# Decoder layer on one core: first two column tiles of the projection multiplied in token halves between the transposes of x

## What is computed

```python
hn = rms_norm(x, mix_norm_w[l])          # x: 1024 x 1024
proj = hn @ w_in[l]                      # w_in: 1024 x 2560
q, k, v, xr, gr = jnp.split(proj, splits, axis=-1)
...                                      # attention on q, k, v; gated recurrence on xr, gr
x = x + jnp.concatenate([att, rnn], axis=-1) @ w_out[l]
hn = rms_norm(x, ffn_norm_w[l])
x = x + hier_moe(hn, ...)                # 32 experts, two for each token
return rms_norm(x, final_norm_w)
```

## Time and profile before

| | us |
|---|---|
| three runs | 1178.47, 1175.91, 1177.88 (median 1177.88) |
| the profiled execution | 1176.9 |
| its span | 1174.8 |
| TensorE busy | 1056.3 (90% of the span) |
| VectorE busy | 878.4 (75%) |
| ScalarE busy | 729.8 (62%) |
| chain of waits, TensorE's share | 59% |
| mean clock granted to TensorE | 0.944 of full |

### The profile page before, as it was taken

How to read it: one execution, slowest core, us unless ns; L and a number is a source line. 1 busy time by engine, 2 the same in 40 slices (tenths; PEclk the granted TensorE clock), 3 DMA queues, 4 the chain that set the end, 5 groups by cost and what they waited for, 6 DMA issues and landing times.

```text
span 1174.8 us, 15610 instructions
## 1 busy us (share of the span) xinstructions
PE 1056.3 (90%) x5171; PEld 870.6 (74%) x5171; DVE 878.4 (75%) x1287; ACT 729.8 (62%) x953; POOL 130.7 (11%) x162
## 2 busy tenths in 40 slices
PE   4899999997777799994999999999999999999950
PEld 3788777786565688883888888888888888888830
DVE  6311266505778777768799999999999999999977
ACT  6222465615656832223688888888888888888824
POOL 1000000000000100001021221221221211211110
PEclk7899999998889999995999999999999999999985
DMA  7111111100004164457599999999999999999577
GB/s 230 52 57 50 37 36 36 36 1 0 1 1 146 21 260 139 144 227 259 214 401 389 375 382 389 381 390 385 366 391 376 370 411 367 385 401 377 226 308 286
DMA packets 49526, 273.27 MB, mean 233 GB/s; under 512 B 12016, under 2 KB 22416, under 8 KB 37200
## 3 DMA queue, kind: packets, MB, share of 16 engines
q1 hardware_dynamic: 40144, 255.72, 55.6%
q0 software_dynamic: 9344, 17.06, 3.9%
HBM read 255.97 MB, written 33.55 MB: 246 GB/s over the span
## 4 chain that ended last, share of the span: by engine, by line
PE 59%; DVE 4%; DMA 1%; issue 0%; ACT 0%; SPq 0%; POOL 0%; POOLq 0%; DVEq 0%
PE ps_moe L68 18%; PE ps_moe L70 17%; PE ps_moe L72 17%; PE ps_moe L1382 2%; PE ps_moe L1184 1%; PE ps_moe L1406 1%; DVE qkvT L1777 1%; DVE gate_up L1754 1%; DVE w_lo L1347 1%; DMA y_d<-y_sb,y_entry 1%; DMA y_second<-y_d 1%; PE ps_moe L1174 1%; PE ps_moe L1167 0%; DVE wout_lo L977 0%; PE ps_moe L1234 0%
## 5 line engine op out<-in xcount | busy, mean ns | idle before, releaser
L1347 DVE TENSOR_TENSOR w_lo<-qkvT,w_hi 128x1024 fp32r<-128x1024 f32 x192 | 224.0, 1224 | 3.7 <-ACT w_hi L1343 1.2
L1343 ACT ACTIVATE w_hi<-qkvT 128x1024 fp32r<-128x1024 f32 x192 | 192.7, 1056 | 15.9 <-PE ps_moe L72 15.9
L68 PE MATMUL ps_moe<-w_hi,x_hi 128*128 128x512 f32 x512 | 162.6, 399 | 4.1 <-DVE x_lo L1391 4.1
L70 PE MATMUL ps_moe<-w_lo,x_hi 128*128 128x512 f32 x512 | 159.3, 392 | 0.0
L72 PE MATMUL ps_moe<-w_hi,x_lo 128*128 128x512 f32 x512 | 158.8, 391 | 0.0
L1347 DVE TENSOR_TENSOR w_lo<-gate_up,w_hi 128x1024 fp32r<-128x1024 f32 x128 | 148.1, 1224 | 2.3 <-ACT w_hi L1343 0.4
L1343 ACT ACTIVATE w_hi<-gate_up 128x1024 fp32r<-128x1024 f32 x128 | 126.4, 1056 | 4.9 <-PE ps_moe L72 4.9
L70 PEld LDWEIGHTS ps_moe<-w_lo,x_hi 128*128 128x128 f32 x512 | 96.9, 189 | 20.9
L72 PEld LDWEIGHTS ps_moe<-w_hi,x_lo 128*128 128x128 f32 x512 | 96.7, 189 | 21.0
L68 PEld LDWEIGHTS ps_moe<-w_hi,x_hi 128*128 128x128 f32 x512 | 94.7, 190 | 22.2 <-DVE x_lo L1391 4.5
L333 DVE TENSOR_TENSOR q_parts<-w_raw,k_parts 128x1024 fp32r<-128x1024 f32 x16 | 19.6, 1224 | 91.9 <-ACT k_parts L233 91.9
(11 more groups left out here) (255 smaller groups left out, 1880.0 us busy)
## 6 DMA issues: line engine op xcount, KB each, us to landing
qkvT<-in_w_exp_gate SPq DMA_DIRECT2D x16, 2048.0 KB, 10.3
qkvT<-in_w_exp_up SPq DMA_DIRECT2D x16, 2048.0 KB, 15.2
gate_up<-in_w_exp_gate SPq DMA_DIRECT2D x16, 2048.0 KB, 10.6
gate_up<-in_w_exp_up SPq DMA_DIRECT2D x16, 2048.0 KB, 15.4
qkvT<-in_w_exp_down SPq DMA_DIRECT2D x16, 2048.0 KB, 14.5
down<-in_w_exp_down SPq DMA_DIRECT2D x16, 2048.0 KB, 14.7
w_raw<-in_w_in SPq DMA_DIRECT2D x10, 1024.0 KB, 5.2
hn_d<-qkvT SPq DMA_DIRECT2D x16, 512.0 KB, 3.8
```

What stands on the lines that cost most here:

```text
L68: nc_mm(o, lh, rh[h], start=start, stop=False)
L70: nc_mm(o, lh, rl[h], start=False, stop=False)
L1343: act.activation(two(w_hi, r), raw_unit(u, par), ACT.Copy).then_inc(q.split_high, 1)
L1347: dve.tensor_tensor(two(w_lo, r), raw_unit(u, par), two(w_hi, r).bitcast(F32), ALU.subtract).then_inc(q.split_low, 1)
```

## The change

1. The load of the norm row moves from SyncE's queue to ScalarE's, ahead of everything that ScalarE does.
2. ScalarE takes one root of a constant before its first square.
3. On ScalarE and VectorE the loops over the x tiles are unrolled. The high and low part of the first weight tile are made behind high and low part 2 of x, those of the second weight tile behind high and low part 4.
4. TensorE transposes x tiles 0 to 4, and then waits for low part 3 (tokens 0 to 511) and the first weight tile. Behind transposes 4 and 5 it multiplies column tile 1 by the first token half, four inner slices (12 products) each time; behind transposes 6 and 7 the same for column tile 2. After the row transpose it multiplies both by the second token half, 24 products each. From the third column tile on the work is as before, its loop of two rounds written out.

The change to lines:

```diff
--- before.py
+++ after.py
@@ -150,7 +150,6 @@
         def _(sp):
             for c in range(2):
                 sp.dma_start(x_sb(c), io["x"][0][c * P:(c + 1) * P, :]).then_inc(x_in[c], 16)
-            sp.dma_start(norm_w[:, :], io["mix_norm_w"][0].partition_broadcast(P)).then_inc(norm_w_in, 16)
             with sp.Fori(1, TT // 2) as i:
                 for c in range(2):
 
@@ -211,7 +210,10 @@
         @block.scalar
         def _(act):
             link = Link(act, act_own)
+            act.dma_start(norm_w[:, :], io["mix_norm_w"][0].partition_broadcast(P)).then_inc(norm_w_in, 16)
             act.wait_ge(ident0, 3)
+
+            link(act.activation(stat[:, 1, 0:1], eps[:, 0:1], ACT.Sqrt))
 
             def square(i, c):
                 act.wait_ge(x_in[c], i * 16 + 16)
@@ -255,21 +257,18 @@
 
             square(0, 0)
             square(0, 1)
-            with act.Fori(0, TT // 2 - 1) as i:
-                link.loop(i, 2)
-                for c in range(2):
-                    square(i + 1, c)
-                    high(i, c)
-            link.end(TT // 2 - 1)
-            split_high((0, 16), 0)
-            high(TT // 2 - 1, 0)
-            high(TT // 2 - 1, 1)
+            for n in range(TT):
+                if n + 2 < TT:
+                    square((n + 2) // 2, n % 2)
+                high(n // 2, n % 2)
+                if n in (2, 4):
+                    split_high((n // 2 - 1, 16), n // 2 - 1)
             act.wait_ge(chan_ready, 2)
             act.activation(soft[:, 2, :], soft[:, 1, :], ACT.Exp, scale=-1.0).then_inc(exp_ready, 1)
-            with act.Fori(0, 2) as i:
-                for c in range(4):
-                    split_high((i * 4 + (c + 1), i * 16 + (16 + 16 * (c == 3))), (c + 1) % 4)
-                    evacuate(i * 4 + c, mixT[:, bass.ds(i * 4 + c, 1)].rearrange("p o n -> p (o n)"), c)
+            for tile in range(8):
+                if tile:
+                    split_high((tile + 1, 16 * ((tile + 1) // 4 + 1)), (tile + 1) % 4)
+                evacuate(tile, mixT[:, tile], tile % 4)
             for i in range(2):
                 for c in range(4):
                     tile = 8 + i * 4 + c
@@ -319,15 +318,6 @@
                                   hT_hi[:, :, at].bitcast(F32), ALU.subtract).then_inc(lo_out, 1)
 
             dve.wait_ge(norm_w_in, 16)
-            scale(0, 0)
-            scale(0, 1)
-            with dve.Fori(0, TT // 2 - 1) as i:
-                link.loop(i, 2)
-                for c in range(2):
-                    scale(i + 1, c)
-                    low(i, c)
-            link.end(TT // 2 - 1)
-
             def split_low(n, c):
                 dve.wait_ge(w_hi_ready, n)
                 ins = dve.tensor_tensor(w_lo[:, c % 2], w_raw[:, c // 2, :, (c % 2) * P:(c % 2 + 1) * P],
@@ -363,9 +353,14 @@
                 dve.tensor_tensor(gate, gate, r_sb[:, :], ALU.mult).then_inc(lru_done, 1)
 
 
-            split_low(1, 0)
-            low(TT // 2 - 1, 0)
-            low(TT // 2 - 1, 1)
+            scale(0, 0)
+            scale(0, 1)
+            for n in range(TT):
+                if n + 2 < TT:
+                    scale((n + 2) // 2, n % 2)
+                low(n // 2, n % 2)
+                if n in (2, 4):
+                    split_low(n // 2, n // 2 - 1)
 
             dve.wait_ge(chan_t, 1)
             dve.tensor_copy(chan[:, :], ps_t[0][:, 0, 0:32]).then_inc(chan_ready, 1)
@@ -390,9 +385,8 @@
                                           op0=ALU.mult, op1=ALU.add))
             link(dve.tensor_scalar(soft[:, 6, :], soft[:, 5, :], 8.0, None, ALU.mult))
             dve.tensor_scalar(soft[:, 7, :], soft[:, 5, :], -8.0, None, ALU.mult).then_inc(soft_ready, 1)
-            with dve.Fori(0, 2) as i:
-                for c in range(4):
-                    split_low(i * 4 + (c + 2), (c + 1) % 4)
+            for tile in range(2, 9):
+                split_low(tile + 1, tile % 4)
             for i in range(2):
                 for c in range(4):
                     if i == 0 or c < 3:
@@ -431,9 +425,20 @@
                                         xn_sb[c][:, k * P:(k + 1) * P], ident[:, :])
                 last.then_inc(turned, 1)
 
-            with pe.Fori(0, TT // 2) as i:
-                turn(i, 0)
-                turn(i, 1)
+            def part(n, c, h, ks):
+                for k in ks:
+                    last = split_products(pe, [ps[c % 2][:, h, :]], w_hi[:, c % 2, k, :], w_lo[:, c % 2, k, :],
+                                          [hT_hi[:, k, h * HALF:(h + 1) * HALF]],
+                                          [hT_lo[:, k, h * HALF:(h + 1) * HALF]], k == 0, k == KT - 1)
+                return last
+
+            for n in range(TT):
+                turn(n // 2, n % 2)
+                if n > 3:
+
+                    pe.wait_ge(lo_out, TT // 2 + 2)
+                    pe.wait_ge(w_lo_ready, n // 2 - 1)
+                    part(n // 2 - 1, n // 2 - 2, 0, range(4 * (n % 2), 4 * (n % 2) + 4))
             pe.wait_ge(lo_out, TT + 2)
             pe.wait_ge(rows_in, 80)
             pe.transpose(ps_t[0][:, 0, 0:32], rows[:, :], ident[0:32, 0:32]).then_inc(chan_t, 1)
@@ -461,9 +466,10 @@
                                          start=True, stop=True)
                 last.then_inc(gates_done, 1)
 
-            with pe.Fori(0, 2) as i:
-                for c in range(4):
-                    tile(i * 4 + (c + 1), c)
+            for c in range(2):
+                part(c + 1, c, 1, range(KT)).then_inc(proj_done, 1)
+            for n in range(3, 9):
+                tile(n, (n - 1) % 4)
             with pe.Fori(0, 2) as i:
                 for c in range(4):
                     tile(i * 4 + (c + 9), c)
```

## The result

The changed kernel took 1179.14 us (median of 18 runs, 1176.64 to 1181.65), the kernel before 1176.83 us in as many runs on the same chips. The ratio is 1.0023, 95% interval 1.0014 to 1.0031: slower by about 2.7 us (2.3 between the medians). One of the 18 runs of the kernel before was far off, at 2210.28 us, and the ratio is of the fast runs alone. The forecast was +3.6 us, slower, 1181.5 us, with the range 1178.7 to 1186.2. The profiled execution of the changed kernel has a span of 1177.3 us, 2.5 above the one before.

A forecast was written before the change was run, and what follows sets the result against it. The prediction took the first weights' landing to set TensorE's start, and column tile 2's end to shift everything after: 0.9 + 2.4 + 0.3 + 0 (clock) = +3.6 us, median 1181.5 us, range 1178.7 to 1186.2.

The forecast's parts named there:

- The mechanism: ScalarE and VectorE stand at the first weight split until the weights land, at 30.27; the shift reaches the end in full.
- The landing: Arrival of the first weight piece, which releases ScalarE's first weight split; taken as unchanged at 30.27 us.
- the weights land earlier: Rival: first weight piece up to 5.8 us earlier, 1175.7 us, so same or faster; chance 0.18.
- From the landing to TensorE's start: Weight split, square 5, root, reciprocal, scale and low part 3 in sequence; TensorE starts at 35.80, not 34.90: +0.9 us.
- Unrolled loops: nothing: Writing out the x-tile loops on ScalarE and VectorE was taken to change the time by nothing.
- Three transpose sets: On TensorE, three sets of eight transposes now follow the start, 0.79 us each: +2.4 us, high end 4.7.
- the restarts behind them: On TensorE, products restarting behind a transpose set cost some 0.1 us each: +0.3 us.
- The clock: TensorE again works 5.3 us at the lower clock level: 0 us, with bounds -0.9 to +0.5.
- The rival of a later rise: TensorE's second group of products and set 5 also run at the lower clock: 3.2 us more, 1184.7 us; chance 0.16.
- No row here shows a rise: Claim that no cited row has TensorE's clock rising just behind a transpose set, except the slowest rise, at 286.0 us.
- The norm row and the root table: At the start, first normalised tile 1 to 2.5 us earlier, hidden by ScalarE's wait for weights: 0 at the end.
- The rival that the change does what it says: Products fill waiting time, some 11 us won, if weights were there at 18 us; given no chance.

The follow-up runs named there:

- w_before_small: The changed kernel with the first two weight loads issued ahead of the nine small loads; 1174.77 us, 0.9981 of the kernel before.
- halves_late: The changed kernel with weight splits behind high and low parts 6 and 7, first-half products behind all transposes; 1173.90 us, 0.9979 of the kernel before.
- w_after_x5: The changed kernel with the first weight load issued behind x tile 5; 1170.03 us, 0.9943 of the kernel before.
- after_again: The changed kernel, unaltered, timed once more on another occasion; 1179.23 us, 1.0023 of the kernel before.
- start_only: The kernel before with only the norm row on ScalarE's queue and the root table loaded first; 1176.01 us, 0.9994 of the kernel before.
- norm_back: The changed kernel with the norm row again behind the first two x tiles on SyncE's queue; 1180.80 us, 1.0037 of the kernel before.
- w_after_x3: The changed kernel with the first weight load behind x tile 3, the second behind x tile 7; 1169.23 us, 0.9937 of the kernel before.
- norm_back_again: The changed kernel with the norm row back on SyncE's queue, timed a second time; 1179.65 us, 1.0014 of the kernel before.

## Why the prediction was right

**The mechanism** was as put: ScalarE in order behind the weight split, the same on VectorE, a stand from about 18 to 29, the shift intact at the end of the projection. w_before_small shows that the end follows the landing; halves_late shows that taking the weight split and the turns out of x's way makes the same halves faster than before.

**The landing** was forecast unchanged at 30.27 and was 28.99 in the profile. The seven profiles with the weights last in the queue spread over 2 us, so a forecast of one profile cannot be better than that; the rival "the weights land earlier" happened in a small part, by scatter and not by the norm row.

**From the landing to TensorE's start** the sum had 5.53 us; six profiles, w_after_x5 with them, show 5.12 or 5.13. The term that was wrong is "Unrolled loops: nothing". The durations were read from x tile 2, in a hardware loop. Written out, the root starts 1.17 after its square (1.28), the reciprocal 0.32 behind it (0.49) and the scale 0.20 behind that (0.33): 0.41 us in sum. The trace of before showed a part of it in its unrolled first tile, where the scale follows the reciprocal by 0.20 (8.41 to 8.61).

**Three transpose sets**, 2.4 us, and the restarts behind them, 0.3: measured 3 x 0.79 = 2.37, and three times 0.08. No set waited for data, and they came at 39.13, 42.77 and 46.39, each as much earlier than forecast as the products had started earlier, within 0.2.

**The clock** was taken at 5.3 us of the lower level from the row transpose on, of which 5.1 us were products; it was 4.7 us of products (34.12 to 38.8), worth -0.2. One profile says little here: with turns the products ran at the lower pace for 3.1 us (after_again) to 5.2 (w_before_small), in the five profiles without turns for 4.7 to 5.2. The means are 3.9 and 4.9 us, so over many runs the term may be nearer -0.5 (an estimate, at 0.2 us for each product). The rival of a later rise did not occur: in all eight profiles with turns the rise came ahead of set 5, in w_before_small only just (near 35.7, the set at 35.74). Sets of 0.79 us between 2.7 us of products left the clock up.

That rival leaned on the Trainium skill ("TensorE: Matmul & The Clock Gate", Part 4: PE-mode transpose), by which transpose work doesn't count as busy for the clock as products do. For these float32 transposes the traces do not agree. TensorE does nothing but transposes until 32.35 in halves_late:

```profile
19.82 1.94 PE L424 MATMUL ps_turn<-ident,scratch 128*128 128x128 f32 x8 [0.58 <-DVE hT_lo L317]
22.34 1.64 PE L424 MATMUL ps_turn<-ident,scratch 128*128 128x128 f32 x8 [0.59 <-DVE hT_lo L317]
24.87 1.06 PE L424 MATMUL ps_turn<-ident,scratch 128*128 128x128 f32 x8 [0.89 <-DVE hT_lo L317]
```

The granted clock is 0.50 at 19 to 22 us, 0.62 at 22 to 24 and 1.00 at 24 to 26: it rose with only transposes before it. The trace of the kernel before had it too, in rows that the prediction does not use: its transposes up to 13.4 us were the first work of TensorE, and the set at 15.86 us took 1.43 us where the next ones took 1.94. So "No row here shows a rise" held for the rows picked and not for the trace, and the rule that gave this rival much of its chance does not hold here.

**The sum** of the measured terms, against the profile of before: landing -1.28, chain 5.13 - 4.63 = +0.50, sets and restarts +2.6, clock -0.2: +1.6, where tile 2's evacuation shows +1.73. With the landing of before it would have been about +3.0, and the timed runs, which average over the landing, say +2.7 by their ratio. So the forecast was 0.6 to 0.9 us high, 0.4 of it for the unrolled loop and 0.2 or more for the clock. The absolute time, 1181.5, was 2.4 high, and 1.05 of that is the base: the three runs that I had gave 1177.88, the 18 give 1176.83. The result lies only 0.4 us above the low end of the range, so it is in part luck that the range held; the sign and the path do not rest on it.

**The norm row and the root table** were costed at nothing, and start_only (0.9994) bears it out. The hidden gain was smaller than the 1 to 2.5 us that I gave: 0.6 us at VectorE's first reciprocal, because the first x tile came 2.0 us later. The prediction kept +1.3 us for such a delay shifting everything behind it; this one did not reach the weights, which were issued at 21.39 against 21.30 in norm_back.

**The rival that the change does what it says** was priced at some 11 us won over the kernel before and given no chance; as the kernel stood, it did not occur. w_after_x3 makes its condition true by moving the load, and wins 7.4 us over the kernel before (9.9 below the changed one), not 11.

## What to carry to other kernels

Before work is pulled ahead under a wait, look at when its operands are issued, not only at when its engine is free: on an in-order engine an early instruction with a late operand takes along everything behind it, here three squares and five high parts of x behind one split. The load has to be moved first, or with it. And once a wait is gone, read what is due next before giving the gain a number; in the old order it was 1.7 us away. And where work is put between others, ask whether the place of its preparation or the work itself brings the gain: the gain of halves_late is as large as what the place of a split explains.

## What the runs showed that I had not expected

The granted clock in the windows is not to be trusted ahead of its first change in a trace. TensorE's windows of norm_back (columns as in the earlier trace rows):

```profile
30.00:38.00 8.00, 3.26 (x8) 1.00 0.04 15
38.00:39.00 1.00, 1.00 (x5) 1.00 0.00 0
```

and its timeline in them:

```profile
37.47 0.63 PE L68 MATMUL ps_proj<-hT_hi,k_parts 128*128 128x512 f32 x1
37.90 0.60 PE L70 MATMUL ps_proj<-hT_lo,k_parts 128*128 128x512 f32 x1
38.33 0.41 PE L72 MATMUL ps_proj<-hT_hi,q_parts 128*128 128x512 f32 x1
38.57 0.40 PE L68 MATMUL ps_proj<-hT_hi,k_parts 128*128 128x512 f32 x1
```

It says 1.00 throughout, yet starts are 0.43 us apart until 38.3 and 0.23 from there, just as in other profiles that show 0.50 and then 1.00. The pace of the products told the clock; the column did not. w_after_x3 shows the same at 24 to 28 us. The mean clock of an execution takes this in: it is 0.956 for norm_back and 0.950 for norm_back_again, the same kernel.

The order of two loads matters to the first consumer even when their bytes are the same: the norm row on a second queue cost the first x tile 2.0 us (6.21 against 4.20), as if the two queues were served side by side. Only that edit separates the two kernels, and nine profiles with the one order and two of norm_back agree; how the DMA engines share the queues was not looked into.

An instruction inside a hardware loop followed its predecessor 0.1 to 0.2 us later than the same instruction written out (0.33 against 0.20 from reciprocal to scale). In the kernel before both forms stand in one trace: 0.20 in its first tile, 0.30 to 0.33 in the loop.
